# Two input blocks begun a token half earlier at the norm transitions, and unread matmuls in gaps of TensorE

## The reference, cut to what matters

```python
# for each of the four sub-layers (mixer 0, FFN 0, mixer 1, FFN 1)
h = rmsnorm(x, g_pre) * (1 + scale) + shift
f = sublayer(h)                    # mixer or ConvFFN
x = x + gate * rmsnorm(f, g_post)
```

## Time and profile before

| what | value |
|---|---|
| median of 3 runs | 1969.06 us (1966.58 to 1976.86) |
| the profiled execution | 1975.2 us, its span 1973.4 us |
| mean granted clock of TensorE | 0.98 |
| busy: PE, PEld | 1848.9 us, 1703.0 us |
| busy: DVE, ACT, POOL | 965.4 us, 844.7 us, 87.4 us |

### The profile page before, as it was taken

How to read it: one execution, slowest core, us unless ns; L and a number is a source line. 1 busy time by engine, 2 the same in 40 slices (tenths; PEclk the granted TensorE clock), 3 DMA queues, 4 the chain that set the end, 5 groups by cost and what they waited for, 6 DMA issues and landing times.

```text
span 1973.4 us, 36003 instructions
## 1 busy us (share of the span) xinstructions
PE 1848.9 (94%) x14644; PEld 1703.0 (86%) x14644; DVE 965.4 (49%) x1558; ACT 844.7 (43%) x1464; POOL 87.4 (4%) x126
## 2 busy tenths in 40 slices
PE   4999988988899999999999899998899999999997
PEld 2999866666788999999999897776799999999997
DVE  4433355455746555325555753434356553255555
ACT  4445322224756444114445643433454442144453
POOL 0000234330000000000000000000000000000000
PEclk9999999899989999999999999999999999999999
DMA  7221455552020222222234311011202222222243
GB/s 278 65 66 54 169 177 186 172 181 85 1 69 22 69 70 82 83 59 74 74 90 134 87 47 44 25 35 33 65 22 64 74 80 76 60 72 74 86 133 112
DMA packets 238716, 170.14 MB, mean 86 GB/s; under 512 B 20138, under 2 KB 230284, under 8 KB 232332
## 3 DMA queue, kind: packets, MB, share of 16 engines
q1 hardware_dynamic: 238604, 168.54, 27.7%
HBM read 165.08 MB, written 3.44 MB: 85 GB/s over the span
## 4 chain that ended last, share of the span: by engine, by line
PE 85%; DVE 6%; ACT 4%; issue 3%; POOL 1%; DMA 0%; SPq 0%; ACTq 0%; DVEq 0%
PE ps L1962 49%; PE ps L2038 12%; PE ps L1995 4%; PE ps L2143 3%; PE ps L2564 2%; PE ps L2148 2%; PE ps L2601 2%; PE ps L2560 2%; PE ps L2293 2%; PE ps L2326 1%; PE ps L2441 1%; PE ps L2418 1%; DVE x_t L1371 1%; ACT w_hi L780 1%; DVE scores L1760 1%
## 5 line engine op out<-in xcount | busy, mean ns | idle before, releaser
L780 ACT ACTIVATE w_hi<-w_raw 128x1024 fp32r<-128x1024 f32 (+4 forms) x193 | 205.1, 1063 | 580.7 <-PE ps L1962 479.4
L1336 DVE TENSOR_TENSOR w_lo<-w_raw,w_hi 128x1024 fp32r<-128x1024 f32 (+4 forms) x197 | 241.6, 1227 | 396.1 <-ACT w_hi L780 395.9
L1962 PE MATMUL ps<-h_hi,w_hi 128*128 128x322 f32 x1744 | 403.6, 313 | 5.3 <-ACT conv L1167 2.5
L1962 PE MATMUL ps<-h_lo,w_hi 128*128 128x322 f32 x1744 | 402.4, 312 | 0.0
L1962 PE MATMUL ps<-h_hi,w_lo 128*128 128x322 f32 x1744 | 400.0, 310 | 0.0
L1962 PEld LDWEIGHTS ps<-h_hi,w_hi 128*128 128x128 f32 x1744 | 294.2, 189 | 7.2 <-DVE w_lo L1336 3.4
L1962 PEld LDWEIGHTS ps<-h_hi,w_lo 128*128 128x128 f32 x1744 | 295.4, 189 | 0.0
L1962 PEld LDWEIGHTS ps<-h_lo,w_hi 128*128 128x128 f32 x1744 | 295.3, 189 | 0.0
L2038 PE MATMUL ps<-g_hi,w_hi 128*128 128x322 f32 x352 | 110.8, 315 | 2.7 <-DVE g_lo L1808 1.6
L2038 PE MATMUL ps<-g_lo,w_hi 128*128 128x322 f32 x352 | 109.4, 311 | 0.0
L2038 PE MATMUL ps<-g_hi,w_lo 128*128 128x322 f32 x352 | 109.2, 310 | 0.0
(11 more groups left out here) (369 smaller groups left out, 3373.6 us busy)
## 6 DMA issues: line engine op xcount, KB each, us to landing
w_raw<-in_ffn_w_up SPq DMA_DIRECT2D x88, 512.0 KB, 3.7
w_mod_raw<-in_w_mod SPq DMA_DIRECT2D x40, 1024.0 KB, 5.8
w_raw<-in_ffn_w_down SPq DMA_DIRECT2D x48, 704.0 KB, 4.2
w_raw<-in_ev_w_in SPq DMA_DIRECT2D x18, 512.0 KB, 3.6
w_mod_first<-in_w_mod SPq DMA_DIRECT2D x8, 1024.0 KB, 15.5
w_raw<-in_ev_w_out SPq DMA_DIRECT2D x8, 512.0 KB, 3.7
w_raw<-in_od_w_out SPq DMA_DIRECT2D x8, 512.0 KB, 3.7
w_raw<-in_od_w_kv_up SPq DMA_DIRECT2D x24, 128.0 KB, 2.3
```

The costliest lines, as they stand in the source:

```text
L780: act.activation(WH[slot][:, 0:k, :], RAW[slot][:, 0:k, :], ACT.Copy).then_inc(w_hi, 1)
L1336: dve.tensor_tensor(WL[slot][:, 0:k, :], RAW[slot][:, 0:k, :], WH[slot][:, 0:k, :].bitcast(F32), ALU.subtract).then_inc(w_lo, 1)
L1962: last = pe.matmul(out, w_of(k, wi), x_of(k, xi, i), start=(k == 0 and p == 0), stop=(k == ks - 1 and p == 2))
```

## The change

At each of the three transitions, blocks 2 and 3 of the next sub-layer are computed in token half 0 right after `second_stat`, and in half 1 after the pair's half 1 (`second_pair`). Their weights go to two resident buffers instead of the two rotating ones, and their results to banks 4 to 7. ACT's copies (`ahead_hi`) and DVE's subtractions of these weights move into the second half of the norm. The rotating buffers then take blocks 4 and 5 directly (`ahead=4`), and block j = 1 of the FFN loop is evacuated from banks 4 to 7. The out-projections use the resident buffers in another order (`res_slot`), so that two of them are free by then. In the odd input projection the statistic of `cq` is issued after block 4 instead of block 3, into banks 6 and 7. POOL's zeroing of the edges of `Gh`, `Gl` waits for block 3 of the FFN instead of the out-projection, and PE waits for it before the down-projection instead of before the loop.

Beside this `keep_busy(b, n)` issues n matmuls of constants (float32, 256 columns) into bank b, whose results nothing reads: 3 before the first `mod_turn` and 12 before `first_pair`; one in each of the last 9 rounds of the even attention and 2 behind it; in the odd attention 2 before each of the last five `c_values`, 3 after one more, and 1 before the out-projection; 2 and 8 around the last `post_stat`. These are 50 in all.

```diff
+    def res_slot(m):
+        return (m + 2) % 6
+    def next_weights(i, u):
+        x = u + (1 if i % 2 else 2)
+        return RESH[x], RESL[x]
...
+            def ahead_hi(i, u):
+                n = N0_OUT[i] + (2 * KD if i % 2 else KD) + u
+                act.wait_ge(w_landed[n % 2], landed_by(n))
+                if i % 2:
+                    act.wait_ge(proj_done, N0_OUT[i] + 2 * KD)
+                else:
+                    act.wait_ge(S("half_done"), 8 * (i // 2) + 4)
+                act.activation(next_weights(i, u)[0][:, :, :], RAW[n % 2][:, 0:KD, :], ACT.Copy).then_inc(w_hi, 1)
+
             def second_half(i, between=None):
                 root(i, "post", 1)
+                ahead_hi(i, 2)
                 for j in range(4):
                     x_square(i, 1, j)
-                    if between and j == 1:
-                        between()
+                    if j == 1:
+                        if between:
+                            between()
+                        ahead_hi(i, 3)
...
-                    body(0, KD)
-                    with act.Fori(1, FH - 1) as j:
+                    if half == 0:
+                        body(0, KD, 4)
+                        body(1, KD, 0, 4)
+                    else:
+                        body(0, KD)
+                    with act.Fori(2 - half, FH - 1) as j:
...
+                for u in (2, 3):
+                    n = N0_OUT[i] + (2 * KD if i % 2 else KD) + u
+                    w = next_weights(i, u)
+                    dve.wait_ge(w_hi, n + 1)
+                    dve.tensor_tensor(w[1][:, :, :], RAW[n % 2][:, 0:KD, :], w[0][:, :, :].bitcast(F32), ALU.subtract).then_inc(w_lo, 1)
                 l, s = SUB[i + 1]
                 dve.wait_ge(*root_ready(i, "pre", 1))
...
                 second_stat(i)
+                if between:
+                    pe.wait_ge(S("c_ctx"), 2)
+                def second_pair(g):
+                    for u in (2, 3):
+                        pe.wait_ge(w_lo, n + u + 1)
+                        for k in range(KD):
+                            last = half_mm(bank(4 + 2 * ((n + u) % 2) + g, HW), next_weights(i, u), (Hh, Hl), k, g, KD)
+                        if g:
+                            last.then_inc(proj_done, 1)
+                second_pair(0)
...
                 for k in range(KD - 2, KD):
                     pair_chunk(n, 1, k, (Hh, Hl), KD, (1,))
+                second_pair(1)
...
+            def keep_busy(b, n):
+                for _ in range(n):
+                    pe.matmul(bank(b, 2 * P), ONES, const(C_ID, 2).rearrange("p c n -> p (c n)"), start=True, stop=True)
...
+            keep_busy(6, 3)
             mod_turn(1, MROW0, 5)
             H = (Hh, Hl)
+            keep_busy(6, 12)
             first_pair(0)
...
+                if u == len(ALLU) - 7:
+                    pe.wait_ge(*of("ln", "on", 8))
+                if u >= len(ALLU) - 7:
+                    keep_busy(7, 1)
...
                     if half == 0:
                         pair_halves(n0, 2 * l)
-                        pe.wait_ge(*filled(f"g_edges{l}"))
-                    with pe.Fori(1 - half, FH) as j:
+                        for b in range(2):
+                            proj(n0 + b + 4, H, free=[evacuated(n0 + b)])
+                    with pe.Fori(3 * (1 - half), FH) as j:
...
-            for m in range(2, 6):
-                proj(N0_ODD_IN + m, H)
-                if m == 3:
-                    norm_stat("cq")
+            for m in range(4, 6):
+                proj(N0_ODD_IN + m, H, free=[evacuated(N0_ODD_IN + m - 4)])
+                if m == 4:
+                    norm_stat("cq", 6)
...
+            keep_busy(4, 2)
             post_stat(3, 1)
+            keep_busy(4, 8)
```

More of the change, by code:

```diff
@@ L788, in squares, with rstd, inverse_root @@
                     act.activation(SQ[k % 2][:, 0:TW], src(k), ACT.Square).then_inc(S("norm_sq"), 1)
-            def rstd(tag, features):
+            def rstd(tag, features, b=4):
                 act.wait_ge(*of("stat", tag, 1))
-                inverse_root(tag, features)
-            def inverse_root(tag, features):
-                act.activation(halves(RST[:, :]), pair(4), ACT.Ln, scale=1.0 / features, bias=EPSC[:, 0:1]
+                inverse_root(tag, features, b)
+            def inverse_root(tag, features, b):
+                act.activation(halves(RST[:, :]), pair(b), ACT.Ln, scale=1.0 / features, bias=EPSC[:, 0:1]
                                ).then_inc(S("norm_ln"), 1)
@@ L1152, in ffn, with body @@
                     v0 = V_FCONV + (3 * l + 1) * 2 * FCH + half * FH
-                    def body(j, ks):
+                    def body(j, ks, ahead=2, b0=0):
                         c = c0 + j
@@ L1159, in body @@
                             act.wait_ge(proj_done, n + 1)
-                            hi(n + 2, slot=slot, k=ks, landed=landed_by(n0 + b + 2) + 16 * j)
+                            if ahead:
+                                hi(n + ahead, slot=slot, k=ks, landed=landed_by(n0 + b + ahead) + 16 * j)
                             if not (isinstance(j, int) and c == 0):
@@ L1165, in body @@
                                 act.wait_ge(S("f_gated"), c)
[L1166 to L1167 removed]
+                            act.activation(halves(U[b][:, :]), pair(b0 + 2 * slot), ACT.Copy).then_inc(S("f_u"), 1)
+                            act.activation(halves(Y[b][:, :]), pair(b0 + 2 * slot), ACT.Copy, scale=vcol(v0 + b * FCH, j)
                                            ).then_inc(evac_a, 1)
@@ L1231, in _ @@
                 act.wait_ge(proj_done, n + 1)
-                hi(n + 2)
+                if m not in (2, 3):
+                    hi(n + (4 if m < 2 else 2))
                 dst = CQ[:, m, :] if m < 3 else CKV[:, m - 3, PAST:KW] if m < 5 else KPT[:, PAST:KW]
-                act.activation(halves(dst), pair(2 * (n % 2)), ACT.Copy).then_inc(evac_a, 1)
+                act.activation(halves(dst), pair(2 * (n % 2) + (4 if m in (2, 3) else 0)), ACT.Copy).then_inc(evac_a, 1)
                 if m == 2:
@@ L1809, in body @@
                                           ALU.subtract).then_inc(S("g_lo_written"), 1)
-                    body(0, KD)
-                    with dve.Fori(1, FH - 1) as j:
+                    if half == 0:
+                        body(0, KD, 4)
+                        body(1, KD, 0)
+                    else:
+                        body(0, KD)
+                    with dve.Fori(2 - half, FH - 1) as j:
                         body(j, KD)
@@ L1881, in _ @@
             ffn(0)
-            for m in range(3):
-                w_rest(N0_ODD_IN + 2 + m)
+            for m in range(2):
+                w_rest(N0_ODD_IN + 4 + m)
             sums("cq", 3)
-            w_rest(N0_ODD_IN + 5)
             dve.wait_ge(*of("rstd", "cq", 1))
```

26 lines of the change are left out of this document (17 added, 9 removed).

## The result

The changed kernel takes **1942.6 us** (median of 4 runs, 1939.7 to 1949.4) beside 1969.7 us for the kernel before: ratio 0.9856, 95% interval 0.9833 to 0.9879, which is 27.1 us less. Measured again beside other kernels it came to 1943.3 us, ratio 0.9860 (0.9844 to 0.9875). The forecast was 1946.5 us, range 1939 to 1957. The profiled execution took 1939.7 us, its span is 1937.9 us.

What follows compares the result with a forecast made beforehand. The time was taken as PE's work, its idle time and its lower-clock stretches. Transitions 18.7 plus unread matmuls 6.8 gave 25.5 us: 1949.7 us from the profiled 1975.2, 1943.6 from the median; middle 1946.5, range 1939 to 1957.

Steps and rivals of the forecast that it cites:

- The transitions: At FFN 0, the odd layer and FFN 1, 144 matmuls run without a wait: gains 6.9, 5.0 and 6.8, together 18.7 us.
- a new wait before `ckv`: At the odd layer's transition, PE waits 1.5 us before the statistic of `ckv`, leaving a gain of 5.0 us there.
- The unread matmuls at their places: 50 unread matmuls in PE's gaps keep its clock full at four places, gaining 6.8 us together.
- The first pair: 12 unread matmuls fit its 5.70 us gap and its 96 matmuls run at full clock: gain 2.6 us.
- out-projection 0: End of even attention: 18 out-projection matmuls and four turns ahead no longer run at half clock: gain 2.7 us.
- Out-projection 1: End of odd attention: about 3.5 us at half clock at this projection's start goes: gain 1.2 us.
- The step that failed: Delta-rule stage: the change leaves it alone, so no gain there; the unread matmuls give 6.8 us in all.
- the middle between profile and median: Whole kernel: 1946.5 us, taken between 1949.7 us reckoned from the profiled run and 1943.6 us from the median.
- Rival 1: Transitions: the chain to half 1 gets later, so they gain 12.7 instead of 18.7 us: 1952.5 us; chance 0.15.
- Rival 2: Changed places: unread matmuls do not hold the clock, or ordinary runs lack half-clock stretches there: 1958 us; chance 0.12.
- Rival 3: FFN loops: each of 36 blocks waits 1.23 us for an evacuation, making the kernel slower: 1988 us; chance 0.02.
- What would show it: Signs: transition gaps gone, block 4 21 to 22 us after the statistic, `ckv` wait, full clock, PE's busy time up.

Runs made afterwards that it cites:

- Number 9: The changed kernel with token half 0 of blocks 2 and 3 put behind half 1 of the first two blocks: 1959.9 us, ratio 0.9951.
- number 3: The kernel before with the 50 unread matmuls, plus 6 more unread ones in each of the three 3-us transition gaps: 1954.8 us, ratio 0.9926.
- number 4: The changed kernel with more unread matmuls (delta-rule stage, even attention's start, before `f_sq`'s wait) and the statistic of `cq` inside block 4: 1944.4 us, ratio 0.9866.
- number 1: The changed kernel without its 50 unread matmuls, the moved matmuls kept: 1955.4 us, ratio 0.9925.
- Number 6: The changed kernel with only the 15 unread matmuls of the first pair: 1948.3 us, ratio 0.9888.
- number 7: The changed kernel with only the unread matmuls at the even attention's end, 9 in its rounds and 2 behind: 1952.4 us, ratio 0.9908.
- number 10: The changed kernel without its unread matmuls, measured once more: 1957.3 us, ratio 0.9931.
- number 8: The changed kernel with only the unread matmuls of the odd attention's end and of the last turns: 1954.9 us, ratio 0.9906.
- number 2: The kernel before with the 50 unread matmuls and nothing else: 1963.4 us, ratio 0.9958.
- number 5: The changed kernel itself, measured again on another occasion beside three other kernels: 1943.3 us, ratio 0.9860.
- number 11: The changed kernel with both ACT copies of the next weights' high parts together, ahead of the squares: 1943.2 us, ratio 0.9867.
- number 12: The changed kernel with the statistic of `cq` inside block 4 and 4 unread matmuls before `f_sq`'s wait: 1943.5 us, ratio 0.9867.

## Why the prediction was right

**The transitions.** Forecast 6.9, 5.0 and 6.8 us; the trace has 7.0, 5.1 and 6.9, by the steps of the prediction: three half-blocks of matmuls without a wait (21.30 us, reckoned 21.46), a new wait before `ckv` (1.11 us, reckoned 1.5). Number 9 shows that the order causes it: undone, it costs 17 us, with the three idle stretches back. All ten traces with the new order have 21.3 us at each of the three transitions. Of the 19 us some 3.5 are clock: in the trace of number 3 the transitions, with the gaps filled by unread matmuls, are 1.4, 0.8 and 1.3 us shorter than before (its median would allow more). Most of the rest is idle time.

**The unread matmuls at their places.** The first pair gained 2.7 us (2.6), out-projection 0 gained 2.3 us, and the turns ahead of it, worth 0.5 us in the sum, gave nothing, for the attention did not get shorter (96.6 us in the mean of the eight traces with unread matmuls at its end, number 4 left out, and 95.1 in the five without, the two groups overlapping). Out-projection 1 gained 1.5 us (1.2), but of four traces without unread matmuls there (numbers 1, 6, 7, 10) none begins that projection at half clock: so this gain is not shown to be the change's. The last turns gained 0.1 us (0.3). One f32 matmul of 256 columns takes 5.35 / 12 = 0.45 us in the first pair (estimated 0.43).

**The step that failed** is the sentence that took the delta-rule stage as left alone, and with it the size of the unread matmuls, 6.8 us. With the moved matmuls in place they are worth 12 to 15 us (numbers 1 and 10 against the change), and the moved ones without them 12 to 15 us too, where I had 18.7: the split of the sum was off on both sides. That the total was near is in part luck. The prediction came out near all the same because its second error had the other sign: I put the middle between profile and median, 3 us above the sum that started from the median (1943.6 us, and 1942.6 was measured). The sum from the median was the better one, and the result does not show that its parts were all right.

**What stands in place of it.** The delta-rule stage is shorter in every kernel that has the first pair's unread matmuls. All five rounds, in the five traces without them (before, numbers 1, 7, 8, 10), take 272.4, 265.1, 267.0, 268.2 and 268.0 us; in the eight with them and none of their own in the stage (after, numbers 2, 3, 5, 6, 9, 11, 12) 257.9, 264.4, 258.6, 259.2, 261.9, 262.8, 260.9 and 261.8 us. The means are 268.1 and 261.0, 7 us apart, and the two groups do not overlap. Over the first four rounds the means are 204.8 and 198.5. Number 6, timed, says the same, 7 us in place of 2.6.

The clock is a part of it: over four rounds it is 0.94, 0.98, 0.97, 0.95 and 0.95 in the first group and 0.97 to 0.99 in the second. It is not all. Numbers 1 and 5 have the same clock in the four rounds and the same busy time of PE to 0.4 us, and still lie 4.6 us apart, in idle time of PE:

```profile
194.28:395.42 201.14, 178.27 (x3090) 142.85 (x3088) 93.64 (x231) 65.91 (x153) 69.33 (x85) 0.98 0.51 181
```

```profile
192.28:388.80 196.52, 177.88 (x3089) 142.90 (x3087) 93.73 (x231) 65.94 (x153) 69.28 (x85) 0.98 0.51 184
```

By what way 15 matmuls at 36 to 44 us act on a stage that begins 150 us later these runs do not show. Its longest regular gaps are the same before and after, four of 1.77 us, and the stage only begins 2.7 us earlier. A kernel that keeps the 15 and begins the stage as late as before would tell a matter of timing from another; it was not tried. It stays open too whether the two parts of the change help each other: the ratios give 0.0072 and 0.0042 for the parts and 0.0142 for the whole, and the rest, 5 us, is about what their intervals leave free.

**The rivals.** *Rival 1* (the chain gets later) is refuted: in the trace of after PE has no idle time over 0.1 us in the 144 matmuls of any transition, the wait before `ckv` is 1.11 us and not 3, and number 11 shows ACT with 1 us to spare. *Rival 2* (the clock terms are not there) is refuted by numbers 1, 2 and 10. What it rested on was right as an observation: the 34 runs of the kernel before beside these experiments spread from 1964.3 to 1976.5 us with their mean granted clock between 0.984 and 0.978. The Trainium skill (TensorE: Matmul & The Clock Gate, "What's actually happening") says that the moment at which the clock changes varies between runs. The runs agree, but the sum over a run varies little: about 0.981 before and 0.992 to 0.996 after in every run, so the clock terms hold in a median. *Rival 3* (the loop loses its lead) appeared as 0.75 us once in each FFN, not in 36 blocks. *Rival 4* did not happen: PE has no wait at the resident half-blocks of FFN 0. *The rule of the Trainium skill on the gap between matmuls* (TensorE: Matmul & The Clock Gate, "Back-to-back issue gap"), which the page gives for a matmul by itself, would have made the transition 19.7 us; it took 21.30.

**What would show it** was right but for one point: PE's busy time did not rise by the unread matmuls, it is 1846.0 us. PE's work at half clock counts as busy too, and less of it is left.

## What to carry to other kernels

Where an engine waits for a norm, move matmuls that need only finished data into the gap: they gain the whole gap, and the clock with it, while unread matmuls in the same gap gained 0.8 to 1.4 us of it in the trace. Unread matmuls paid where the gap could not be filled with work (numbers 2 and 6), and gained nothing in the delta-rule stage (number 4); a trace with a better clock is no faster by itself. Price the clock from several executions, since a stage that the change leaves alone can hold the largest difference between two traces.

## What the runs showed of the hardware that I had not expected

- **A stretch at half clock costs less than half of itself.** Over the 34 runs of before, a fit of time on the time at half clock (span x 2 x (1 - clock)) gives 0.37 us per us, correlation 0.87; PE alone would give 0.5. Removing the last of it gained nothing (number 4: clock 0.996 to 0.999 in its runs, 1944.4 us).
- **The clock can drop behind a gap of 1.77 us, and the same gap need not be followed by a drop.** Each trace but number 4's has four such gaps in the delta-rule stage, all with the same work around them. In after the clock fell behind one, in before behind three, in the 13 traces behind 17 of 52. Two of them in after, and the 4 us behind each (the last three numbers are the clock, the DMA share and GB/s):

```profile
279.40 0.27 PE L2370 MATMUL ps<-consts,level_b 64*64 64x64 f32 x2 [1.77 <-POOL level_b L737]
...
325.53 0.27 PE L2370 MATMUL ps<-consts,level_b 64*64 64x64 f32 x2 [1.77 <-POOL level_b L737]
```

```profile
281.00:285.00 4.00, 4.00 (x58) 1.94 (x52) 1.92 (x4) 0.00 (x0) 4.00 (x5) 0.57 0.03 6
327.00:331.00 4.00, 4.00 (x84) 2.14 (x80) 1.83 (x5) 1.12 (x4) 4.00 (x5) 1.00 0.22 37
```

Of the 3-us gaps at the transitions each of nine was followed by half clock, in before and in numbers 2 and 9. So a short gap can be priced only as a chance, from several traces.
